# Borders between the stages of a hybrid decoder kernel: order of the last gate stores, early constants, weight loads inside the merge

## Chip, cores, metric

One core of a Trainium2 chip runs the whole program. The metric is the time of one execution in microseconds on the device; several timed runs are made of each kernel, and one further execution is profiled.

## What is computed

One layer of a decoder with three parallel branches, for a prompt of 2048 tokens and a sample group of 8 requests with 8 tokens each (2112 tokens in all, model width 1024, fp32). Cut to what matters here:

```python
h = rms_norm(x, p['norm_g'])
z = h @ p['w_in']                       # 1024 -> 7200 columns
a_x, a_g, b_s, b_g, c_q, c_kv, c_pe, c_g, gate_logits = split(z)
o_a = rg_lru(causal_conv(a_x)) * silu(a_g)        # branch a: RG-LRU, width 512
o_b = rwkv7_mix(b_s) * silu(b_g)                  # branch b: RWKV-7 recurrence, width 512
o_c = attend(q, ckv, c_pe) * silu(c_g)            # branch c: latent attention, width 512
g_a, g_b, g_c = split(sigmoid(gate_logits))       # three gates of 1024 columns
merged = g_a * (o_a @ w_oa) + g_b * (o_b @ w_ob) + g_c * (o_c @ w_oc)
y = x + merged @ w_out
```

The states of the branches (the last hidden state, convolution inputs, shifted columns, the recurrence's matrix states, the latents) are outputs too.

## The kernel before

Five engines run instruction streams of their own and meet through semaphores: PE (matmul), DVE and ACT (elementwise), POOL (elementwise and some transfers), SP (nearly all transfers). The program is a row of phases; each ends with a barrier over all engines (`Phase.__exit__`, L61), and SP reaches it only after the waits at the end of its own stream. Intermediate results go through DRAM between the phases: `zT` (branch inputs), `gT` (24 gate tiles of 128 columns), `oaT`, `obT`, `ocT` (branch outputs), `mT` (merged).

**Projection** (`trunk_phase`, L138). The tiles of 128 columns of z are worked on in pairs; each pair is computed by seven half-size products instead of eight (`ORDER`, L147), and DVE adds each product to the quarters of the two tiles that it belongs to (`adds`, L531; a quarter is one tile for one half of the tokens, 1056 of them). The last pairs are gate tiles: when both halves of a tile are summed, ACT makes tanh of the 2112 columns (`mix`, L387) and SP stores the tile (`store`, L248). After the loop over the pairs SP waits for DVE's copies of the branch states, issues 9 + 16 small stores of states (L270 to L280), stores the last two gate tiles (L281, L282), and waits until they have landed (L285).

**Prompt attention** (`prompt_attention_phase`, L1045) loads a pair of heads' keys into `kh` (two buffers, L1054) before PE's first score (L1180). **Sample attention** (`sample_attention_phase`, L1400) works through the eight requests; SP only loads a few new keys there (L1465 to L1470) and stores the result.

**Recurrence** (`rwkv_phase`, L1783). Twenty chunks (four per pair of heads, then the samples) go through a software pipeline, written out by hand per engine (`frame`). At its start SP issues 15 constants (L1891 to L1898; `lvl_f` are the level masks, cast by POOL at L1977, the others parameters and masks), then the three activations of chunk 0 (`load_inputs`, L1900), the low-rank input `wa` (1 MB for the prompt, L1951, and the sample columns, L1953), then both finished branches for the merge (`branches.load`, L2666, 4.2 MB each), then the activations of chunk 1. PE waits for all constants and for `prep` (L2044, L2045), that is for POOL's preparation, then multiplies `wa` (L2228). ACT waits for `prep` (L2327), squares the keys (L2335) and then takes PE's result (L2342, the log decay), on which everything else of the chunk hangs.

**Merge** (`merge_phase`, L2669). For each of 8 blocks of 128 columns, 15 units: three branches times five chunks of 424 tokens (the last 416). A unit is four matmuls into one of eight PSUM banks; DVE multiplies it by the gate (L2749) and adds it up (L2753). The weights of a block (three 256 KB matrices, one semaphore for all three, L2696) and its three gates (1056 KB each, L2700) have two buffers. POOL loads the recurrence's output, which the third branch needs (L2715).

**Output** (`out_phase`, L2756). Pairs of 128 tokens, seven products again; DVE makes sums of the token tiles (L2892) and, once, DVE and POOL make five sums of quarters of `w_out` (L2899, L2879). SP issues the first tokens (L2799), then the four quarters of `w_out` (1 MB each, L2811), then rows of x (L2806).

Of the kernel before, what the change touches and what calls it, by code (L numbers as in the profile page):

```python
# [12 lines left out]
P = 128  # L13
# [7 lines left out]
W = 512  # L21
# [116 lines left out]
def trunk_phase(nc, A, O, hT, ident, zT, gT, oaT, later, ahead):  # L138
# [15 lines left out]
    UPTO = {2: 2, 5: 4, 1: 6, 7: 7, 6: 8}  # L154
    with Phase(nc, "z") as p:
# [78 lines left out]
        with nc.Block() as block:  # L234
            @block.sync
            def _(sp):
# [24 lines left out]
                for q in range(NQ + 1):  # L261
                    if q:
# [18 lines left out]
                store(NQ, 0)  # L281
                store(NQ, 1)  # L282
                sp.wait_ge(xm_out, 16 * len(mixed))
                for u in range(4):
                    sp.wait_ge(st_out[u], 16 * max(stores[n] for q, r, n in ALL if buf(q, r) == u))  # L285
# [88 lines left out]
            def _(act):  # L374
# [85 lines left out]
                mix(NQ, 0)  # L460
                mix(NQ, 1)
# [583 lines left out]
def prompt_attention_phase(nc, A, O, ident, zT, qT, kT, v_d, ocT, outs, data):  # L1045
# [6 lines left out]
    with Phase(nc, "a") as p:  # L1052
        qb = p.sb("qb", [QK, 4, 2, P])
        kh = p.sb("kh", [QK, 2, 2, T])  # L1054
# [44 lines left out]
        with nc.Block() as block:  # L1099
            @block.sync  # L1100
            def _(sp):
                def heads(j):
                    for e in range(2):
                        sp.dma_start(kh[:, j % 2, e], kT[2 * j + e, :, 0:T]).then_inc(k_in[j % 2], 16)
# [64 lines left out]
            def _(pe):  # L1169
                def score(n, c):  # L1170
# [9 lines left out]
                    nc.tensor.matmul(S[x % 3][:, 0:cols], qb[:, m % 4, e], kh[:, j % 2, e, c * W:c * W + cols],  # L1180
# [219 lines left out]
def sample_attention_phase(nc, A, O, ident, ocT, data):  # L1400
# [4 lines left out]
    with Phase(nc, "s") as p:  # L1405
# [377 lines left out]
def rwkv_phase(nc, A, O, ident, zT, obT, oaT, ocT, branches):  # L1783
# [11 lines left out]
    with Phase(nc, "r") as p:  # L1795
        masks = p.sb("masks", [P, 4, C])
        lvl = p.sb("lvl", [P, LEVELS, 2, C], mybir.dt.uint8)
        bones = p.sb("bones", [P, P])
        cen = p.sb("cen", [P, P])
        bones2 = p.sb("bones2", [P, 2])  # L1800
        ident2 = p.sb("ident2", [P, C])
        scanm = p.sb("scanm", [P, W])
        prm = p.sb("prm", [P, 8, 4])
        tiny = p.sb("tiny", [P, 4])
        lora = p.sb("lora", [P, 4, P])
        wa = p.sb("wa", [P, T + W])
# [37 lines left out]
        c_in, prep, wa_in = p.sem("c_in"), p.sem("prep"), p.sem("wa_in")  # L1844
# [42 lines left out]
        with nc.Block() as block:  # L1887
            @block.sync
            def _(sp):
                cols = lambda a: a.rearrange("(q p) -> p q", p=P)  # L1890
                for dst, src in ((masks[:], A["rw_masks"]), (lvl_f, A["rw_levels"]), (bones[:], A["rw_bones"]),  # L1891
                                 (bones2[:], A["rw_bones2"]), (ident2[:], A["rw_ident2"]), (scanm[:], A["rw_scanm"]),
# [776 lines left out]
def merge_phase(nc, A, gT, obT, mT, branches):  # L2669

    with Phase(nc, "m") as p:
# [16 lines left out]
        with nc.Block() as block:  # L2688
            @block.sync
            def _(sp):  # L2690
                def loads(n):
# [5 lines left out]
                    if n >= 2:  # L2697
                        sp.wait_ge(took, NU * (n - 1))
# [312 lines left out]
```

## Time and profile before

| | |
|---|---|
| three timed runs | 4051.89, 4056.64, 4057.94 us; median 4056.64 |
| profiled execution | 4046.41 us |
| its span, first to last instruction | 4044.6 us |
| mean granted clock of PE | 0.967 of full |
| busy: PE, DVE, ACT, POOL | 92%, 51%, 33%, 11% of the span |
| moved by DMA | 293.48 MB |

A busy share is an average over all phases. The granted clock is the share of the full 2.4 GHz that the chip let PE have; 0.5 is its lower level. The start times below are microseconds from the first instruction.

### The profile page before, as it was taken

The numbers are of one execution on the slowest core, as the hardware profiler recorded it, in microseconds if no ns is written. First come the engines' busy times: TensorE is split into PE (matmuls) and PEld (weight loads), VectorE is DVE, ScalarE is ACT, GpSimd is POOL, SyncE is SP. The second block draws the span as 40 slices with busy tenths as digits, with TensorE's granted clock in tenths as the row PEclk, the third lists the DMA queues.
The fourth block names the chain that finished last, engine by engine and source line by source line (L and its number), as shares of the span: only waits on it lengthen the run. The fifth ranks groups of instructions, "written<-read, shape, count | busy, mean of one in ns | idle before, by whom it ended". The sixth has DMA issues, their size and how long they took to land. (4 is left out here: it accounts for less than half of the span.)

```text
span 4044.6 us, 72368 instructions
## 1 busy us (share of the span) xinstructions
PE 3723.9 (92%) x30307; PEld 2430.9 (60%) x30307; DVE 2076.8 (51%) x3717; ACT 1344.1 (33%) x2324; POOL 426.2 (11%) x580
## 2 busy tenths in 40 slices
PE   7879999999999999779999799977999998799899
PEld 4546666666666666456666555555777777455444
DVE  5863234444333333355666577764666664233353
ACT  4431012232233232244455455543555544000000
POOL 1000000000000000021111323302111121000000
PEclk9989999999999999899999899988999999899999
DMA  4422112222222222331211111003111111423342
GB/s 148 115 67 59 65 64 80 75 78 80 74 79 68 76 74 72 87 97 52 53 30 30 34 53 53 22 9 137 37 43 43 43 27 27 177 102 128 113 141 91
DMA packets 270300, 293.48 MB, mean 73 GB/s; under 512 B 81765, under 2 KB 229114, under 8 KB 255642
## 3 DMA queue, kind: packets, MB, share of 16 engines
q1 hardware_dynamic: 261066, 246.38, 19.6%
q0 software_dynamic: 8912, 42.48, 3.1%
q8 instruction: 242, 3.96, 0.4%
q14 instruction: 80, 0.66, 0.1%
HBM read 181.38 MB, written 107.42 MB: 71 GB/s over the span
## 5 line engine op out<-in xcount | busy, mean ns | idle before, releaser
L325 PE MATMUL z_acc<-z_hx,ahead_ws 128*128 128x352 f32 x1872 | 558.0, 459 | 0.0
L543 DVE TENSOR_TENSOR z_st<-z_st,z_acc 128x1056 f32<-128x1056 f32 x208 | 253.9, 1252 | 589.3 <-PE z_acc L325 589.3
L325 PEld LDWEIGHTS z_acc<-z_hx,ahead_ws 128*128 128x128 f32 x1872 | 355.7, 190 | 198.1
L325 PE MATMUL z_acc<-hT,ahead_ws 128*128 128x352 f32 x1248 | 376.9, 459 | 0.0
L325 PE MATMUL z_acc<-hT,ahead_wt 128*128 128x352 f32 x1248 | 373.4, 459 | 0.0
L1180 PE MATMUL a_S<-a_kh,a_qb 96*128 96x512 f32 (+3 forms) x640 | 289.5, 548 | 52.3 <-DMA a_kh<-kT 27.9
L325 PEld LDWEIGHTS z_acc<-hT,ahead_ws 128*128 128x128 f32 x1248 | 236.8, 190 | 135.5 <-issue 7.7
L325 PEld LDWEIGHTS z_acc<-hT,ahead_wt 128*128 128x128 f32 x1248 | 237.1, 190 | 132.1
L1528 PE MATMUL s_kn<-sd_wuk,s_ckT 128*128 128x512 f32 x528 | 287.9, 627 | 22.1 <-issue 17.0
L415 ACT ACTIVATE z_st<-z_acc 128x1056 f32<-128x1056 f32 x104 | 103.6, 1048 | 449.0 <-PE z_acc L325 449.0
L2729 PE MATMUL m_acc<-branches_o,m_wb 128*128 128x424 f32 (+1 forms) x640 | 230.1, 521 | 23.4 <-DMA m_wb<-in_w_ob 23.4
L2729 PEld LDWEIGHTS m_acc<-branches_o,m_wb 128*128 128x128 f32 x640 | 122.3, 191 | 129.7 <-issue 106.0
L1257 DVE CUSTOM_DVE_ANT_0 a_pr_l<-a_S,a_zm 128x512 f32<-128x512 f32 (+2 forms) x224 | 138.1, 629 | 117.6 <-PE a_S L1180 117.3
L1606 ACT ACTIVATE s_sq<-s_kn 128x512 f32<-128x512 f32 x264 | 155.9, 597 | 104.1 <-PE s_kn L1528 104.0
L1529 PEld LDWEIGHTS s_scp<-s_qabs,s_ckT 128*128 128x128 f32 x528 | 102.0, 193 | 129.8 <-issue 129.8
L1655 DVE TENSOR_REDUCE s_ssk<-s_sq 128x32 f32<-128x2048 f32 (+1 forms) x72 | 151.2, 2101 | 10.2 <-ACT s_sq L1606 9.8
L1180 PEld LDWEIGHTS a_S<-a_kh,a_qb 96*128 96x128 f32 x640 | 106.3, 202 | 79.2 <-issue 49.7
L1230 ACT ACTIVATE a_pr_l<-a_pr_l,a_nm 128x1024 f32<-128x1024 f32 (+7 forms) x128 | 122.5, 957 | 74.2 <-DVE a_nm L1264 58.7
L1189 PEld LDWEIGHTS a_tb<-ident,a_pr_l 128*128 128x128 f32 x800 | 98.2, 143 | 79.5 <-issue 58.9
L397 ACT ACTIVATE z_st<-z_st 128x2112 f32<-128x2112 f32 x24 | 47.1, 1964 | 271.4 <-DVE z_st L543 271.4
L1189 PE MATMUL a_tb<-ident,a_pr_l 128*128 128x128 f32 x800 | 117.8, 276 | 11.0 <-DVE a_pt_l L1220 9.9
L350 POOL DMA_DIRECT2D oaT<-z_tr x19 | 10.6, 558 | 1090.8 <-DVEq L598 1090.8
(411 smaller groups left out, 6389.4 us busy)
## 6 DMA issues: line engine op xcount, KB each, us to landing
ahead_wt<-in_w_in SPq DMA_DIRECT2D x52, 512.0 KB, 5.1
gT<-z_st SPq DMA_DIRECT2D x24, 1056.0 KB, 5.3
m_sg<-gT SPq DMA_DIRECT2D x24, 1056.0 KB, 9.2
zT<-z_xm SPq DMA_DIRECT2D x17, 1056.0 KB, 4.0
zT<-z_st SPq DMA_DIRECT2D x12, 1056.0 KB, 6.9
r_xs<-zT SPq DMA_DIRECT2D x48, 256.0 KB, 3.3
mT<-m_macc SPq DMA_DIRECT2D x8, 1056.0 KB, 5.4
p_xin<-in_x_prompt SPq DMA_DIRECT2D x16, 512.0 KB, 4.1
```

The costliest lines, as they stand in the source:

```text
L325: last = nc.tensor.matmul(acc[slot][:, i, 0:CH3], w[:, k], HB[m][:, k, i * CH3:(i + 1) * CH3], start=(k == 0), stop=(k == KH - 1))
L415: last = f(half(q, r, c), src, ACT.Copy)
L543: tt(y, y, src, ALU.add if sign > 0 else ALU.subtract).then_inc(took_v, 1)
L1180: nc.tensor.matmul(S[x % 3][:, 0:cols], qb[:, m % 4, e], kh[:, j % 2, e, c * W:c * W + cols], start=True, stop=True).then_inc(scored, 1)
L1189: last = nc.tensor.transpose(tb[x % 3][:, q], probs(n)[:, (4 * c + q) * P:(4 * c + q + 1) * P], ident[:])
L1230: nc.scalar.activation(probs(n)[:, k0:k1], probs(n)[:, k0:k1], ACT.Exp, bias=nm[:, n % 4:n % 4 + 1], accum_out=ls[:, n // 2 % 2, n % 2, c ...
L1257: nc.vector.tensor_tensor_reduce(out=probs(n)[:, c * W:c * W + cols], in0=S[x % 3][:, 0:cols], in1=mask, scale=1.0, scalar=NEG, op0=ALU.ad ...
L1528: nc.tensor.matmul(kn[page % 3][:], ckT[:, r, q], wuk[:], start=True, stop=True).then_inc(kn_done, 1)
L1529: nc.tensor.matmul(scp[r][:, q], ckT[:, r, q], qabs[:, b:b + 1].rearrange("p a n -> p (a n)"), start=(q == 0), stop=False, skip_group_chec ...
L1606: nc.scalar.activation(sq[:, r, q], kn[page % 3][:], ACT.Square).then_inc(squared, 1)
L1655: nc.vector.tensor_reduce(own, sq[:, r, 0:k].rearrange("p a (h d) -> p a h d", h=H), AX.X, ALU.add).then_inc(summed, 1)
L2729: last = nc.tensor.matmul(acc[x % 8][:, 0:tn], wb[:, n % 2, k, q], o[k][:, q, t0:t0 + tn], start=(q == 0), stop=(q == 3))
```

## The change

Four edits at the borders of the phases:

1. The last pair's tanh and stores are made by quarters (tile, half of the tokens), each as soon as its last add is done; the small stores of states come after them. Before the barrier SP waits for the quarters.
2. A buffer of 16 KB per partition, `early.pool`, lives from prompt attention to the end. First it holds one of the two key buffers; at the start of the sample phase, 14 of the 15 constants of the recurrence and the prompt's part of `wa` are loaded into it. The level masks stay in the recurrence, behind the activations of chunk 0. PE's wait for POOL's preparation moves to its first statistics product.
3. In the merge each weight matrix has a semaphore of its own; gates go through a ring of four slots, each loaded when the gate four places before it is used up; one of the two sums lies in `early.pool`.
4. The four quarters of `w_out` are loaded into a buffer of their own (`last.wo`) during the merge, after the store of its fourth block; the output's token sums lie where the branches were.

```diff
+    QUARTERS = ((1, 0), (0, 1), (0, 0), (1, 1))
+    LAST_ADD = {(1, 0): 1, (0, 1): 3, (0, 0): 7, (1, 1): 8}
...
+                for x, (r, c) in enumerate(QUARTERS):
+                    sp.wait_ge(gate_r, len(gates) - 2 + x + 1)
+                    u, t0 = buf(NQ, r), 1 + c * HALF
+                    sp.dma_start(gT[tiles(NQ)[r] - 29, :, c * HALF:(c + 1) * HALF], st[:, u, t0:t0 + HALF]).then_inc(st_out[u], 16)
                 sp.wait_ge(sh_cp, 1)
...
-                store(NQ, 0)
-                store(NQ, 1)
...
-                mix(NQ, 0)
-                mix(NQ, 1)
+                for r, c in QUARTERS:
+                    act.wait_ge(took_v, 8 * (NQ - 1) + LAST_ADD[r, c])
+                    t0 = 1 + c * HALF
+                    part = st[:, buf(NQ, r), t0:t0 + HALF]
+                    f(part, part, ACT.Tanh, scale=0.5).then_inc(gate_r, 1)
...
-        kh = p.sb("kh", [QK, 2, 2, T])
+        kh = [early.keys(), p.sb("kh", [QK, 2, T])]
...
                 sp.wait_ge(const_set, 2)
+                early.load(sp, A, zT)
...
+class Early:
...
+        self.pool = ctx.enter_context(nc.sbuf_tensor("early_pool", [P, 2 * T], F32))
...
+    def load(self, sp, A, zT):
...
+        for dst, src in ((self.masks, A["rw_masks"]), (self.bones, A["rw_bones"]),
...
+            sp.dma_start(dst, src, allow_slow_non_contiguous=True).then_inc(self.c_in, 16)
+        sp.dma_start(self.wa[:, 0:T], zT[20, :, 1:T + 1]).then_inc(self.wa_in, 16)
...
-                for dst, src in ((masks[:], A["rw_masks"]), (lvl_f, A["rw_levels"]), (bones[:], A["rw_bones"]),
...
-                    sp.dma_start(dst, src, allow_slow_non_contiguous=True).then_inc(c_in, 16)
...
                 load_inputs(0)
-                sp.dma_start(wa[:, 0:T], zT[20, :, 1:T + 1]).then_inc(wa_in, 16)
+                sp.dma_start(lvl_f, A["rw_levels"]).then_inc(lvl_in, 16)
                 sp.wait_ge(prep, 1)
...
-                g.wait_ge(c_in, 15 * 16)
+                g.wait_ge(c_in, 14 * 16)
+                g.wait_ge(lvl_in, 16)
...
-                pe.wait_ge(c_in, 15 * 16)
-                pe.wait_ge(prep, 5)
+                pe.wait_ge(c_in, 14 * 16)
...
                 def input_stats(n):
+                    if n == 0:
+                        pe.wait_ge(prep, 5)
...
-        sg = p.sb("sg", [P, 2, 3, TT])
+        sg = p.sb("sg", [P, 4, TT])
-        macc = p.sb("macc", [P, 2, TT])
+        macc = [early.pool[:, 0:TT], p.sb("macc", [P, TT])[:]]
...
+                def weights(n):
+                    if n >= KD:
+                        return
                     u = n % 2
                     if n >= 2:
                         sp.wait_ge(prod, NU * (n - 1))
                     for k, w in enumerate((A["w_oa"], A["w_oc"], A["w_ob"])):
-                        sp.dma_start(wb[:, u, k], w[0].rearrange("(k p) n -> p k n", p=P)[:, :, n * P:n * P + P]).then_inc(w_in[u], 16)
...
+                        sp.dma_start(wb[:, u, k], w[0].rearrange("(k p) n -> p k n", p=P)[:, :, n * P:n * P + P]).then_inc(w_in[u][k], 16)
+
+                def gate(x):
+                    if x >= 3 * KD:
+                        return
+                    if x >= 4:
+                        sp.wait_ge(took, 5 * (x - 3))
+                    sp.dma_start(sg[:, x % 4], gT[ORDER[x % 3] * KD + x // 3]).then_inc(g_in[x % 4], 16)
+
+                weights(0)
+                for x in range(3):
+                    gate(x)
+                sp.wait_ge(prod, 5)
+                weights(1)
+                gate(3)
+                for n in range(KD):
                     for k in range(3):
...
+                        gate(3 * n + k + 4)
+                    weights(n + 2)
                     sp.wait_ge(m_r, 10 * (n + 1))
...
+                    sp.dma_start(mT[n], macc[n % 2]).then_inc(stored[n % 2], 16)
+                    if n == 3:
+                        last.load(sp, A)
...
-                    pe.wait_ge(w_in[n % 2], 48 * (n // 2 + 1))
...
+                        if c == 0:
+                            pe.wait_ge(w_in[n % 2][k], 16 * (n // 2 + 1))
...
-        wo = p.sb("wo", [P, KD, D])
+        wo, wo_in = last.wo, last.wo_in
-        ms = p.sb("ms", [P, 2, 5, KH, P])
+        ms = branches.o[:, 0].rearrange("p k t -> p (k t)")[:, 0:10 * KH * P].rearrange("p (u a k n) -> p u a k n", u=2, a=5, k=KH)
...
                 load_m(0)
-                for q in (0, 3, 1, 2):
-                    r, c = q // 2, q % 2
-                    sp.dma_start(B(r, c), A["w_out"][0, r * W:(r + 1) * W, c * W:(c + 1) * W].rearrange("(k p) n -> p k n", p=P)).then_inc(wo_in[q], 16)
                 load_x(0)
```

## Rows read from the trace of the kernel before

**Rows 1.** The page, part 1: PE's busy time, share of the span, instructions.

```profile
PE 3723.9 (92%) x30307; PEld 2430.9 (60%) x30307; DVE 2076.8 (51%) x3717; ACT 1344.1 (33%) x2324; POOL 426.2 (11%) x580
```

**Rows 2.** Windows view: stretch, length, busy (records) by engine, granted clock, DMA.

```profile
3473.00:3480.00 7.00, 6.30 (x13) 3.30 (x14) 0.60 (x1) 0.00 (x0) 0.00 (x0) 0.69 0.81 338
3480.00:3600.00 120.00, 120.00 (x340) 64.29 (x339) 41.71 (x70) 0.00 (x0) 0.00 (x0) 1.00 0.34 120
```

**Rows 3.** Timeline, projection to prompt attention: start, us, engine, line [idle before <-releaser].

```profile
1650.40 1.25 DVE L543 TENSOR_TENSOR z_st<-z_st,z_acc 128x1056 f32<-128x1056 f32 x1 [5.85 <-PE z_acc L325]
...
1651.69 1.96 ACT L397 ACTIVATE z_st<-z_st 128x2112 f32<-128x2112 f32 x1 [5.13 <-DVE z_st L543]
...
1652.08 0.40 SPq L273 DMA_DIRECT2D out_p_shift<-later_shT  x1
...
1660.86 0.83 SPq L256 DMA_DIRECT2D gT<-z_st  x2
...
1678.73 10.89 PE L1180 MATMUL a_S<-a_kh,a_qb 96*128 96x512 f32 x20 [27.92 <-DMA a_kh<-kT]
```

**Rows 4.** SP's waits, 1640 to 1690: us in total, times, longest.

```profile
SPq L285 <- DMA gT<-z_st: 5.7, 2, 3.1
```

**Rows 5.** Timeline, sample attention to recurrence.

```profile
2725.85 0.35 SPq L1898 DMA_DIRECT2D r_masks<-in_rw_masks  x1
...
2733.59 1.52 SPq L1910 DMA_DIRECT2D r_xs<-zT  x3
...
2735.88 0.82 POOL L1977 CAST r_lvl<-r_GM 128x768 uint8<-128x768 f32 x1 [7.66 <-DMA r_lora<-in_rw_a]
...
2739.91 0.72 ACT L2335 ACTIVATE r_sq<-r_xs,r_prm 128x512 f32<-128x512 f32 x1 [27.71 <-DMA r_xs<-zT]
...
2743.38 2.04 PE L2228 MATMUL r_r<-r_wa,r_lora 64*128 64x512 f32 x2 [22.01 <-DMA r_wa<-zT]
2745.46 0.69 ACT L2342 ACTIVATE r_lw<-r_r,r_prm 128x512 f32<-128x512 f32 x1 [4.82 <-PE r_r L2228]
```

**Rows 6.** Timeline, recurrence to merge.

```profile
3455.61 0.37 SPq L2696 DMA_DIRECT2D m_wb<-in_w_oa  x1
...
3457.12 2.31 SPq L2700 DMA_DIRECT2D m_sg<-gT  x3
...
3473.70 30.43 PE L2729 MATMUL m_acc<-branches_o,m_wb 128*128 128x424 f32 x80 [23.37 <-DMA m_wb<-in_w_ob]
...
3478.74 0.60 DVE L2749 SCALAR_TENSOR_TENSOR m_macc<-m_sg,m_acc 128x424 f32<-128x424 f32 x1 [26.58 <-PE m_acc L2729]
```

**Rows 7.** DMA view, 3452 to 3476: issues, KB each, median us from issue to landing.

```profile
m_ob<-obT POOLq DMA_DIRECT2D x1, 4224.0 KB, 17.4
m_sg<-gT SPq DMA_DIRECT2D x3, 1056.0 KB, 20.9
m_wb<-in_w_oa SPq DMA_DIRECT2D x1, 256.0 KB, 3.2
m_wb<-in_w_oc SPq DMA_DIRECT2D x1, 256.0 KB, 5.1
m_wb<-in_w_ob SPq DMA_DIRECT2D x1, 256.0 KB, 17.1
```

**Rows 8.** Timeline, merge to output.

```profile
3828.35 3.10 DVE L2892 TENSOR_TENSOR y_ms<-y_mb 128x512 f32<-128x512 f32 x5 [11.01 <-DMA y_mb<-mT]
...
3831.38 9.28 PE L2863 MATMUL y_acc<-y_wo,y_ms 128*128 128x512 f32 x16 [15.28 <-DMA y_wo<-in_w_out]
```

**Rows 9.** DMA view, 2722 to 2745.

```profile
r_GM<-in_rw_levels SPq DMA_DIRECT2D x1, 384.0 KB, 3.0
...
r_wa<-zT SPq DMA_DIRECT2D x1, 32.0 KB, 7.3
```

**Rows 10.** DMA view of the whole program: medians from issue to landing.

```profile
m_sg<-gT SPq DMA_DIRECT2D x24, 1056.0 KB, 9.2
...
y_wo<-in_w_out SPq DMA_DIRECT2D x4, 1024.0 KB, 10.2
```

More of the change, by code:

```diff
@@ L2666, in load, with __init__, merge_phase @@
             eng.dma_start(self.o[:, k], src.rearrange("n p t -> p n t")).then_inc(self.o_in[k], 16)
-def merge_phase(nc, A, gT, obT, mT, branches):
+class Last:
+    def __init__(self, nc, ctx):
+        self.wo = ctx.enter_context(nc.sbuf_tensor("last_wo", [P, KD, D], F32))
+        self.wo_in = [ctx.enter_context(nc.semaphore(f"last_wo_in{k}")) for k in range(4)]
+    def load(self, eng, A):
+        KH = KD // 2
+        for q in (0, 3, 1, 2):
+            r, c = q // 2, q % 2
+            eng.dma_start(self.wo[:, KH * r:KH * r + KH, W * c:W * c + W],
+                          A["w_out"][0, r * W:(r + 1) * W, c * W:(c + 1) * W].rearrange("(k p) n -> p k n", p=P)).then_inc(self.wo_in[q], 16)
+def merge_phase(nc, A, gT, obT, mT, branches, early, last):
     with Phase(nc, "m") as p:
@@ L2681, in merge_phase @@
         ORDER = (0, 2, 1)
-        g_in = [p.sems(f"g{u}_in", 3) for u in range(2)]
-        w_in, stored = p.sems("w_in"), p.sems("st")
+        g_in = p.sems("g_in", 4)
+        w_in, stored = [p.sems(f"w{u}_in", 3) for u in range(2)], p.sems("st")
         prod, took, m_r = p.sem("prod"), p.sem("took"), p.sem("mr")
@@ L2753, in _, with out_phase @@
                             nc.vector.tensor_tensor(m, m, out, ALU.add).then_inc(m_r, 1)
-def out_phase(nc, A, O, mT, outs):
+def out_phase(nc, A, O, mT, outs, branches, last):
     KH = KD // 2
@@ L2954, in build @@
             trunk_phase(nc, A, O, hT, ident, zT, gT, oaT, later, ahead)
-        with ExitStack() as middle:
-            data = SampleData(nc, middle)
-            prompt_attention_phase(nc, A, O, ident, zT, qT, kT, v_d, ocT, later.outs, data)
-            sample_attention_phase(nc, A, O, ident, ocT, data)
-        with ExitStack() as back:
-            branches = Branches(nc, back)
-            rwkv_phase(nc, A, O, ident, zT, obT, oaT, ocT, branches)
-            merge_phase(nc, A, gT, obT, mT, branches)
-        out_phase(nc, A, O, mT, later.outs)
+        with ExitStack() as around:
+            early = Early(nc, around)
+            with ExitStack() as middle:
+                data = SampleData(nc, middle)
+                prompt_attention_phase(nc, A, O, ident, zT, qT, kT, v_d, ocT, later.outs, data, early)
+                sample_attention_phase(nc, A, O, ident, zT, ocT, data, early)
+            with ExitStack() as back:
+                branches = Branches(nc, back)
+                rwkv_phase(nc, A, O, ident, zT, obT, oaT, ocT, branches, early)
+                last = Last(nc, back)
+                merge_phase(nc, A, gT, obT, mT, branches, early, last)
+                out_phase(nc, A, O, mT, later.outs, branches, last)
 OUT = {"y_p": (1, T, D), "y_s": (DB, TS, D), "p_lru_h": (1, 1, 512), "p_lru_conv": (1, 1, 3, 512),
```

74 lines of the change are left out of this document (36 added, 38 removed).

## The prediction

> **What bounds the kernel now.** I read the page first: TensorE (PE) is busy for 92% of the span [rows 1], so time can only be won where PE stands idle or where a phase is one chain of small steps. The windows view says that the merge is full once it runs: 120 us busy of 120, at the full granted clock, 340 matmul records; eight of them make one unit (one branch, 424 tokens), so a unit takes 120 / 340 x 8 = 2.82 us [rows 2]. Inside the phases the change has nothing to win; I therefore read the timeline at the borders, and beside it the DMA view and SP's waits. Four borders can be seen to stand still.
>
> At the first (projection to prompt attention) SP issues 25 small stores and only then the last two gate tiles, and must see those landed before the barrier: small stores from 1652.08, gates at 1660.86, PE again at 1678.73 [rows 3]; SP's waits put 5.7 us to the gates' landing [rows 4]. At the third (sample to recurrence) SP issues 15 constants before the first activations: POOL casts the masks when the last constant is there, ACT starts on the activations 4.03 us later, PE starts when the low-rank input is in, and the chain's first elementwise result is ACT's at 2745.46 [rows 5]. At the fourth (recurrence to merge) PE starts at 3473.70, on the last of three weight matrices [rows 6]; the first had taken 3.2 us and the third 17.1 [rows 7]. At the fifth (merge to output) PE waits for output weights until 3831.38, though the tokens were there at 3828.35 [rows 8].
>
> **The change, part by part.** The sum is made against the profiled execution: span 4044.6 us, 4046.41 us in all. That is 10.2 us under the median of the timed runs, 4056.64; I carry the difference in microseconds over to the median.
>
> *First border.* Before, SP is free when the gates have landed: 1660.86 + 0.83 + 5.7 = 1667.4 [rows 3, 4]. After, three quarters are stored while PE still works. The last needs the last add (ends 1651.65) and a tanh over half the elements: half of 1.96, so 1651.69 + 0.98 = 1652.67 [rows 3]. Its issue takes half of 0.83, 0.4 us, and then come the small stores, 1660.86 - 1652.08 = 8.8 us: SP ends at 1661.9, and the quarter lands behind that work (5.7 us for four times the bytes bounds it). Nobody waits for the small stores before the end of prompt attention. Gain 1667.4 - 1661.9 = 5.5 us; between 4.0, if issuing beside a store is slower, and 6.5. The next loads then run as they do now. The additional ACT instructions lie under the adds.
>
> *Second border.* 14 constants and the 1 MB low-rank input are issued by SP when the sample phase has set its own constants: about 7.7 us of issue, as now from 2725.85 to 2733.59 [rows 5]. Queued behind them on SP are the new keys of the third request, which wait for the first request's sums anyway. Cost nothing; without that cover, 7.7 us. The two halves of the prompt's keys only change address: nothing.
>
> *Third border.* SP begins with the three activation loads (1.52 us of issue), then the level masks at about 2727.4, the sample columns at about 2727.9, then both branches. POOL, whose queue holds the cast and what follows, now waits for the level masks. The trace has no such transfer behind three 256 KB loads. The bounds are 3.0 us (the same masks, nearly alone) and 7.3 us (the sample columns behind 1.8 MB) [rows 9]; I take 4.8, nearer the lower end, since 768 KB lie in front. So masks at 2732.2. Cast to ACT's first square is 4.03 us and from there to the log decay 0.72 and a gap of 0.02 [rows 5], hence 2732.2 + 4.8 = 2737.0 in place of 2745.46: gain 8.5 us, between 6.0 and 10.3. PE's first product may be as late as 2727.9 + 7.3 + 2.1 = 2737.3 without undoing this. The wait for the other POOL work, moved to PE's statistics, comes later than ACT's own wait for the same and costs nothing.
>
> *Fourth border.* PE now waits for one matrix at a time. The first lands at 3455.61 + 3.2 = 3458.8 [rows 6, 7]: gain 3473.70 - 3458.8 = 14.9 us. Does it last? The first unit takes 3478.74 - 3473.70 = 5.0 us on the slow start (granted clock 0.69 of full in these 7 us, a mixture of 1.2 and 2.4 GHz) [rows 2, 6]. PE can fill eight banks before DVE must free one: until 3458.8 + 5.0 + 7 x 2.82 = 3483.5. DVE needs the gates: the median one lands 20.9 us after an issue near 3457.6, so 3478.5 [rows 6, 7]. The second matrix had taken 5.1 us and is needed after five units, at 3475; the third matrix and the recurrence's output (17.1 and 17.4 us) are there by 3473.7, when PE starts now, and needed after ten units, at 3489. No stall: 14.9 us. Lower bound, if the first matrix lands like the second: 13.
>
> A rule speaks against this step. The Trainium skill (DMA: Bandwidth & Descriptors, section Queues, rings and completion order) says that each DMA engine takes turns between the queues that have work, a packet at a time, and that completion does not follow the order of issue. By that rule the first matrix could be caught by POOL's 4.2 MB as the third was; the sum would be 16.4 us instead of 31.3. The trace agrees for the third matrix and not for the first.
>
> In the merge, gates go through four slots instead of six. A gate is issued when the one four before it is used up, three gates or 15 x 2.82 = 42 us ahead of need, and takes 9.2 us [rows 10]: nothing. The 4 MB of output weights go out after the fourth block's store, ahead of later gates on SP: 4 us of issue, and even four median landings in a row, 41 us [rows 10], end, with the gate behind them, within the 56 us that the next gate has (20 units): nothing. The separate weight waits on PE are satisfied by then: nothing.
>
> *Fifth border.* The weights are there, so PE starts on the first token sum: 3828.35 plus a fifth of 3.10, 3829.0 [rows 8]; gain 2.4 us, between 1.5 and 3.5 (the tokens now have other loads behind them). What would be late next are the three weight sums on DVE and two on POOL; they move earlier by more than PE does.
>
> Sum: 5.5 + 8.5 + 14.9 + 2.4 = 31.3 us. Span 4013.3, from the median 4025.3.
>
> **The rivals.** *First matrix late.* If the engines spread POOL's transfer over it, PE starts at 3473.5 as before, and 14.9 us are lost: 4056.64 - 16.4 = 4040.2. Against it stands the row of 3.2 us, with the same issues in the same order; for it the row of 17.1 [rows 7].
>
> *Next inputs late.* The second chunk's activations stand on SP behind 8.4 MB of branches, and ACT's chain may wait for these instead of the masks, so that the 8.5 us are given back at the second chunk: 4033.8. Against it: the branches are issued about 8 us earlier as well, and so are these.
>
> *Both.* Only the first and fifth borders remain, 7.9 us: 4048.7, which the measurement cannot tell from no change (0.2%, 8.1 us).
>
> *Slower: four slots.* If gates should land so late that DVE and then PE wait at each of the 20 gates that recycle a slot, the merge loses. It starts to lose beyond 42 us from issue to landing, and loses more than everything won from 42 + 31.3 / 20 = 43.6 us; at 44.1 us it is 20 x 2.1 = 42 us lost, 10.7 us slower: 4067.3. Against it: 9.2 us [rows 10]; even beside the 4.2 MB transfer the median was 20.9 [rows 7].
>
> **How the numbers follow.** Forecast 0.72; first matrix late 0.12; next inputs late 0.06; both 0.06; four slots 0.04. Faster by over 0.2%: 0.72 + 0.12 + 0.06 = 0.90; same 0.06; slower 0.04. The likeliest case gives 4025.3; with its terms at their best ends (6.5 + 10.3 + 14.9 + 3.5 = 35.2) 4021.4, and with the timed runs' downward spread of 4.75 us and some 2.5 us for a PE that starts at full clock after a shorter gap, 4014. The upper end takes in the late first matrix, 4040.2, and the runs' upward spread of 1.3: 4042.
>
> **What would show it.** In the new timeline: SP's first load of prompt attention about 5.5 us closer to the last add; the cast on POOL about 6.4 us after SP's first issue of the recurrence, not 10.0; the merge's first matmul about 3.3 us after SP's first weight issue, not 18.1, and no idle PE until the ninth unit; the output's first matmul 0.7 us after the first token sum begins, and a DMA share above the old one in the sample's first slices only. Wrong would be: a merge that starts with the third matrix, PE gaps at the ninth unit, a second chunk that begins no earlier, or a slower merge between its borders.

## The result, and the profile after

| | before | after |
|---|---|---|
| median of the timed runs | 4054.26 us (4 runs, 4049.48 to 4057.94) | 4019.45 us (4 runs, 4015.89 to 4025.47) |
| ratio | | 0.9916, 95% interval 0.9899 to 0.9934 |
| profiled execution, and its span | 4046.41, 4044.6 us | 4021.59, 4019.8 us |
| a later comparison of the same two (9 and 5 runs) | 4047.93 us | 4024.44 us, ratio 0.9946 (0.9932 to 0.9960) |

The change makes the kernel faster: 34.8 us by the medians of the first comparison, 24.8 by the two profiled spans, 23.5 in the later comparison. The forecast was 31.3. Why three measurements of one change differ by 11 us turned out to be the larger question; the kernel before alone gives medians of 4047.93 and 4054.26 here, and the changed one 4019.45 and 4024.44. First the borders.

**First border.** Timeline of the changed kernel, as in [rows 3] (start, us, engine, line, what, idle before).

```profile
1649.05 1.25 DVE L551 TENSOR_TENSOR z_st<-z_st,z_acc 128x1056 f32<-128x1056 f32 x1 [5.85 <-PE z_acc L330]
...
1651.44 0.32 SPq L275 DMA_DIRECT2D gT<-z_st  x1
1651.81 0.46 SPq L279 DMA_DIRECT2D out_p_shift<-later_shT  x1
...
1660.64 0.30 SPq L286 DMA_DIRECT2D out_s_lru_conv<-later_lruT  x1
1662.18 0.33 SPq L1119 DMA_DIRECT2D a_qb<-qT  x1
...
1673.31 11.09 PE L1188 MATMUL a_S<-early_pool,a_qb 96*128 96x512 f32 x20 [23.86 <-DMA early_pool<-kT]
```

The last quarter goes out before the small stores, and SP reaches its first load 13.13 us after the start of the last add instead of 18.15. PE's first score comes 24.26 us after it, 4.07 earlier than before (28.33). What fills the border now is SP's issue of small stores, 1651.81 to 1660.94.

**Third border.** Timeline, as in [rows 5].

```profile
2717.35 0.42 DVE L1742 SCALAR_TENSOR_TENSOR s_oS<-s_oS,sd_cg 128x256 f32<-128x256 f32 x1
...
2720.86 1.30 SPq L1937 DMA_DIRECT2D r_xs<-zT  x3
...
2726.91 0.82 POOL L2005 CAST r_lvl<-r_GM 128x768 uint8<-128x768 f32 x1 [3.70 <-DMA r_GM<-in_rw_levels]
...
2730.33 0.72 ACT L2364 ACTIVATE r_sq<-r_xs,early_pool 128x512 f32<-128x512 f32 x1 [23.16 <-POOL early_pool L2012]
2730.96 0.67 ACT L2371 ACTIVATE r_lw<-r_r,early_pool 128x512 f32<-128x512 f32 x1
```

The cast starts 6.05 us after SP's first issue instead of 10.03, and the first log decay 13.61 us after the last elementwise instruction of the sample phase (2717.35) instead of 23.10.

**Fourth and fifth border.** First the timeline at the merge's start, as in [rows 6]; then the DMA view of 3446 to 3460, as in [rows 7]; then the timeline at the output's start, as in [rows 8].

```profile
3447.24 0.38 SPq L2742 DMA_DIRECT2D m_wb<-in_w_oa  x1
...
3452.21 18.09 PE L2785 MATMUL m_acc<-branches_o,m_wb 128*128 128x424 f32 x46 [10.24 <-DMA m_wb<-in_w_oa]
3467.37 2.61 DVE L2805 SCALAR_TENSOR_TENSOR early_pool<-m_sg,m_acc 128x424 f32<-128x424 f32 x5 [23.57 <-DMA m_sg<-gT]
```

```profile
m_wb<-in_w_oa SPq DMA_DIRECT2D x1, 256.0 KB, 4.9
m_wb<-in_w_oc SPq DMA_DIRECT2D x1, 256.0 KB, 5.2
m_wb<-in_w_ob SPq DMA_DIRECT2D x1, 256.0 KB, 16.7
```

```profile
3806.50 3.10 DVE L2944 TENSOR_TENSOR branches_o<-y_mb 128x512 f32<-128x512 f32 x5 [10.94 <-DMA y_mb<-mT]
3807.25 5.18 PE L2915 MATMUL y_acc<-last_wo,branches_o 128*128 128x512 f32 x8 [12.94 <-DVE branches_o L2944]
```

PE now starts on the first matrix, 4.97 us after SP's first weight issue instead of 18.09. DVE waits for the gates until 3467.37, and PE fills its banks meanwhile and does not stop. The output starts 0.75 us into the first token sums; before, it waited 3.03 us for weights.

The ledger is read from the same instruction in both profiles (after minus before, us):

| instruction | shift | what the stretch gave |
|---|---|---|
| projection's last add | -1.35 | nothing changed so far: two executions |
| first score | -5.42 | -4.07, first border |
| last elementwise instruction of the sample phase | -5.01 | +0.41 |
| first log decay (chunk 1) | -14.50 | -9.49, third border |
| log decay of chunk 3 | -6.35 | **+8.15** |
| last store of the recurrence | -8.37 | -2.02 |
| merge's first product | -21.49 | -13.12, fourth border |
| merge's last add | -21.78 | -0.29 |
| output's first product | -24.13 | -2.35, fifth border |
| end of the span | -24.8 | -0.67 |

The row in bold is not in the forecast: two chunks after the third border, 8.15 of the 9.49 us are gone. The reason shows when the granted clock is read there. Below is ACT's timeline in the kernel before, chunks 2 and 3, and then the windows view (stretch, length, busy and records of PE, weight loads, DVE, ACT, POOL, then the granted clock).

```profile
2769.76 0.69 ACT L2342 ACTIVATE r_lw<-r_r,r_prm 128x512 f32<-128x512 f32 x1 [3.31 <-PE r_r L2228]
...
2801.17 0.69 ACT L2342 ACTIVATE r_lw<-r_r,r_prm 128x512 f32<-128x512 f32 x1 [5.54 <-PE r_r L2228]
```

```profile
2755.00:2766.00 11.00, 5.43 (x66) 3.75 (x68) 4.02 (x6) 0.37 (x2) 2.62 (x2) 0.50 0.86 350
2768.00:2773.00 5.00, 4.95 (x132) 3.16 (x132) 2.96 (x5) 2.36 (x4) 0.75 (x1) 1.00 0.00 0
```

The same two views of the changed kernel:

```profile
2756.64 0.69 ACT L2371 ACTIVATE r_lw<-r_r,early_pool 128x512 f32<-128x512 f32 x1 [5.28 <-PE r_r L2255]
...
2794.82 0.69 ACT L2371 ACTIVATE r_lw<-r_r,early_pool 128x512 f32<-128x512 f32 x1 [5.55 <-PE r_r L2255]
```

```profile
2755.00:2766.00 11.00, 10.18 (x136) 6.75 (x136) 4.63 (x8) 5.03 (x8) 2.15 (x2) 0.50 0.01 1
2766.00:2772.00 6.00, 6.00 (x100) 5.53 (x100) 1.96 (x3) 1.51 (x3) 0.38 (x1) 0.50 0.01 3
2774.00:2790.00 16.00, 14.23 (x414) 12.20 (x414) 9.45 (x15) 8.02 (x12) 3.31 (x3) 1.00 0.16 52
```

Behind chunk 2's log decay stand level products (those of chunk 1, as the pipeline is written). Before, PE reached them at 2769.66, just after the full clock (2.4 GHz) had come at 2767.4. After, it reaches them at 2756.53, 13 us sooner by the trace's time and 8 us sooner counted from the end of the sample phase, and does them at 0.50, the lower level, until 2772.6: 38.18 us from chunk 2 to chunk 3 instead of 31.41. That is 6.78 of the 8.15 us; the other 1.37 go in chunk 1, which is at half clock in both kernels. The head start is spent at half speed, and the full clock even comes later than before: 55.3 us after the sample phase's last elementwise instruction instead of 45.0.

### The profile page after: what moved, and what is told of

It reads as the page before. It is cut to its first block and busy times, and to the rows that moved or that the text cites. A ratio compares the mean times of both kernels' runs of the same rounds, so it can differ in the third digit from the quotient of the medians.

```text
span 4019.8 us, 72387 instructions
## 1 busy us (share of the span) xinstructions
PE 3727.5 (93%) x30307; PEld 2434.0 (61%) x30307; DVE 2075.6 (52%) x3717; ACT 1344.9 (33%) x2326; POOL 426.3 (11%) x580
## 5 line engine op out<-in xcount | busy, mean ns | idle before, releaser
L1188 PE MATMUL a_S<-early_pool,a_qb 96*128 96x512 f32 (+3 forms) x320 | 147.9, 560 | 45.3 <-DMA early_pool<-kT 23.9
L1188 PE MATMUL a_S<-a_kh,a_qb 96*128 96x512 f32 (+3 forms) x320 | 141.5, 535 | 3.9 <-DMA a_qb<-qT 3.9
```

The source lines that it names most:

```text
L1188: nc.tensor.matmul(S[x % 3][:, 0:cols], qb[:, m % 4, e], kh[j % 2][:, e, c * W:c * W + cols], start=True, stop=True).then_inc(scored, 1)
```

## The experiments

All are edits of the changed kernel, except where it is said. The table holds what each profile shows: PE's first score after the start of the projection's last add; the log decays of chunks 1 and 3 after the sample phase's last elementwise instruction; the time from the third to the twentieth log decay; the merge's first product after SP's first weight issue; and the timed runs (ratio to the kernel before on the same chip). The kernel called late here is the one with late constants.

| kernel | score | chunk 1 | chunk 3 | 3rd to 20th | merge | median us | ratio (95%) |
|---|---|---|---|---|---|---|---|
| before | 28.33 | 23.10 | 78.81 | 572.69 | 18.09 | | 1 |
| after | 24.26 | 13.61 | 77.47 | 568.90 | 4.97 | 4019.45 | 0.9916 (0.9899 to 0.9934) |
| after, again | 23.42 | 13.72 | 77.49 | 568.75 | 4.26 | 4024.44 | 0.9946 (0.9932 to 0.9960) |
| all weights | 23.21 | 13.65 | 77.50 | 570.48 | 18.27 | 4037.91 | 0.9965 (0.9951 to 0.9979) |
| late | 23.68 | 23.20 | 78.92 | 577.69 | 2.92 | 4028.47 | 0.9944 (0.9928 to 0.9961) |
| busy PE | 23.47 | 13.61 | 67.47 | 570.64 | 2.74 | 4012.18 | 0.9908 (0.9892 to 0.9925) |
| late and busy PE | 23.60 | 25.61 | 81.08 | 570.51 | 2.95 | 4025.39 | 0.9942 (0.9927 to 0.9958) |
| states early | 16.29 | 14.46 | 77.98 | 581.34 | 4.57 | 4020.22 | 0.9921 (0.9905 to 0.9938) |
| statistics apart | 23.26 | 13.65 | 74.65 | 556.11 | 2.80 | 4000.79 | 0.9886 (0.9871 to 0.9901) |
| statistics apart, again | 23.47 | 13.85 | 77.53 | 556.23 | 2.75 | 3999.73 | 0.9874 (0.9857 to 0.9891) |
| late, statistics apart | 23.50 | 22.62 | 78.34 | 556.23 | 4.42 | 4004.15 | 0.9890 (0.9875 to 0.9905) |
| before, statistics apart | 28.76 | 22.37 | 78.14 | 557.76 | 17.29 | 4024.89 | 0.9941 (0.9927 to 0.9954) |
| three edits together | 16.00 | 13.96 | 67.76 | 555.13 | 2.95 | 3983.17 | 0.9839 (0.9825 to 0.9852) |

**All weights: is it the third matrix that held PE?**

```diff
-                        if c == 0:
-                            pe.wait_ge(w_in[n % 2][k], 16 * (n // 2 + 1))
+                        if c == 0 and k == 0:
+                            for j in range(3):
+                                pe.wait_ge(w_in[n % 2][j], 16 * (n // 2 + 1))
```

> The changed kernel, but PE waits for all three weight matrices of a block before the block's first product, as before the change. Theory (the third matrix was what held PE at the fourth border): the merge's first product comes about 17 to 18 us after SP's first weight issue instead of 4.97, and the time rises by 12 to 13 us, to about 4032. Rival (the first gates, which land 20 us after that issue, set the merge's pace, so that an early PE only fills its banks): the first product is as late, but the merge ends at most 3 us later, about 4020 to 4022.

Timeline and DMA view of this kernel at the merge's start:

```profile
3449.76 0.38 SPq L2742 DMA_DIRECT2D m_wb<-in_w_oa  x1
...
3468.03 4.22 PE L2786 MATMUL m_acc<-branches_o,m_wb 128*128 128x424 f32 x6 [23.54 <-DMA m_wb<-in_w_ob]
```

```profile
m_wb<-in_w_oa SPq DMA_DIRECT2D x1, 256.0 KB, 2.7
m_wb<-in_w_oc SPq DMA_DIRECT2D x1, 256.0 KB, 12.3
m_wb<-in_w_ob SPq DMA_DIRECT2D x1, 256.0 KB, 17.1
```

It was: PE starts at 18.27, when the third matrix is there, although the first had taken 2.7 us. From SP's first weight issue to the merge's last add it takes 361.33 us, against 347.73 with separate waits and 361.14 before. So 13.4 to 13.6 us arrive at the merge's end, and the rival, by which the gates set the pace, falls. The median stands 18.5 and 13.5 us above the two of the changed kernel, which were not run beside it; the theory had 12 to 13, and its 4032 was 6 us too low.

**Late: what are the early constants worth?** The call moves out of the sample phase, back to the head of the recurrence.

```diff
-                early.load(sp, A, zT)
...
+                sp.dma_start(lvl_f, A["rw_levels"]).then_inc(lvl_in, 16)
+                early.load(sp, A, zT)
                 load_inputs(0)
-                sp.dma_start(lvl_f, A["rw_levels"]).then_inc(lvl_in, 16)
+                sp.dma_start(wa[:, 0:T], zT[20, :, 1:T + 1]).then_inc(wa_in, 16)
```

> The changed kernel, but the 14 constants and the 1 MB of low-rank input are issued in the recurrence again, in the old order (constants and level masks, activations, low-rank input). Theory (the second chunk runs at half the clock until a moment that the earlier start does not move, so most of the third border's gain is given back there): the first log decay is 9 us later after the last elementwise instruction of the sample phase (23 instead of 13.6), but the third chunk's log decay only 1 to 2 us later (about 79 instead of 77.5), and the time 4020 to 4022. Rival (the 9.5 us of the border are kept and what was lost in the recurrence is chance): the third chunk's log decay at 86 to 87, the time about 4029.

The profile says what the theory said: chunk 1 is 9.6 us later, chunk 3 only 1.45. The time says 4028.5, the rival's number; but its ratio, 0.9944, is that of the unaltered changed kernel in the later comparison, 0.9946. By time alone this run decides nothing. In its profile another 8.8 us are lost between the third and the twentieth log decay, where the edit does nothing. One part of the theory does not hold: the moment of the full clock moves with the edit. It comes 45.0 us after the sample phase's last elementwise instruction here, as before the change, and 55.3 with early constants.

**Busy PE: is it the clock?** Throwaway products fill PE's gaps in chunk 1.

```diff
+                def warm(*cols):
+                    for n in cols:
+                        mm(go[:, 0:n], ident[:], scanm[:, 0:n], start=True, stop=True)
...
                 def lora_w(n):
                     if n == 0:
+                        warm(W, W, W, W)
```

There are five more such calls, ahead of the second low-rank product (640 columns), the input's statistics (256), the bonus (1024), the scales (256) and the two halves of the gram products (1024 and 256).

> The changed kernel, with throwaway products on PE in the gaps of the recurrence's first chunk (the identity times the scan mask, into a bank that nobody has read yet): about 8 us of them before the first low-rank product and 0.5 to 4 us in each later gap. Theory (PE's half clock holds the second chunk): PE is granted the full clock within some 7 us of the phase's start, as after the first border, and the third chunk's log decay comes 66 to 71 us after the last elementwise instruction of the sample phase instead of 77.5; the time falls by 7 to 11 us, to 4008 to 4013. Rival one (the second chunk waits for its activations, which stand behind both branches): 77 and no change, 4019. Rival two (the clock does not answer, and the added products delay the chain by the part that does not fit the gaps): 79 to 82, 4021 to 4024.

Windows view of this kernel from the end of the sample phase, and ACT's log decays of chunks 2 and 3:

```profile
2721.00:2726.00 5.00, 4.19 (x6) 1.87 (x7) 0.00 (x0) 0.00 (x0) 2.37 (x5) 0.53 0.61 193
2726.00:2733.00 7.00, 4.22 (x11) 1.72 (x10) 0.31 (x1) 1.30 (x2) 3.15 (x10) 0.97 1.05 372
2733.00:2743.00 10.00, 10.00 (x20) 4.78 (x19) 4.93 (x8) 6.71 (x10) 3.15 (x3) 0.51 1.01 427
2743.00:2790.00 47.00, 40.03 (x1078) 31.41 (x1076) 28.04 (x46) 19.29 (x30) 9.76 (x8) 1.00 0.21 80
```

```profile
2754.34 0.69 ACT L2385 ACTIVATE r_lw<-r_r,early_pool 128x512 f32<-128x512 f32 x1 [2.06 <-PE r_r L2262]
...
2785.75 0.69 ACT L2385 ACTIVATE r_lw<-r_r,early_pool 128x512 f32<-128x512 f32 x1 [5.54 <-PE r_r L2262]
```

The full clock comes with the throwaway products (1.00 from 2743 on, against 2772), and with it chunk 3 comes 10.0 us sooner. The time, 4012.18, lies in the theory's 4008 to 4013. The next activations still stand behind both branches here, so "next inputs late" is out as the cause, and the products added delay nothing that can be seen.

**Late and busy PE: the border's worth with the clock out of the way.** The two edits together, the throwaway products now identity times identity and three times as many at the start.

```diff
-                        mm(go[:, 0:n], ident[:], scanm[:, 0:n], start=True, stop=True)
+                        for _ in range(n // P):
+                            mm(go[:, 0:P], ident[:], ident[:], start=True, stop=True)
...
-                        warm(W, W, W, W)
+                        warm(*[W] * 12)
+                        pe.wait_ge(c_in, 14 * 16)
```

> The changed kernel with the constants and the low-rank input loaded in the recurrence again, as in the kernel with late constants, and throwaway products on PE from the phase's start, here identity times identity, as long as the constants take, and in the gaps of the first chunk. Theory (the early constants are worth 9.5 us, and PE's half clock in the second chunk hid most of it): with the clock up in both, the third chunk's log decay comes about 9.5 us later than in the kernel with busy PE (77 against 67.5 us after the last elementwise instruction of the sample phase), and the time is about 9 us above that kernel's 4012, 4021. Rival (early constants are worth 1.4 us whatever the clock): 69, and 4013 to 4014.

PE's timeline at the first low-rank product, and the windows view of the two stretches behind it:

```profile
2743.29 2.04 PE L2263 MATMUL r_r<-early_pool 64*128 64x512 f32 x2 [6.90 <-DMA early_pool<-zT]
```

```profile
2742.00:2758.00 16.00, 14.71 (x46) 10.47 (x47) 5.15 (x8) 7.40 (x11) 3.14 (x3) 0.50 1.01 423
2759.00:2801.00 42.00, 35.97 (x983) 29.90 (x982) 24.66 (x39) 16.31 (x26) 8.48 (x7) 1.00 0.14 46
```

Chunk 3 comes at 81.08, 13.6 us after the kernel with early constants and busy PE. That is more than the 9.5 expected, for two reasons. Chunk 1 itself is 12.0 us later: its low-rank input landed 2.4 us later than in the late kernel (the sample columns took 9.9 us from issue to landing, 7.5 there), and PE stood idle for it for 6.90 us, behind the throwaway products. And after this gap chunk 1 runs at half clock again, 24.06 us to chunk 2's log decay instead of 22.46. From chunk 2 to chunk 3, at the full clock in both, each takes 31.41 us. So the 12.0 us of chunk 1 are all still there at chunk 3 where PE is fast in chunk 2, and only 1.45 of 9.6 where it is not. The rival's 69 us is out. The time, 4025.39, is 13.2 us above busy PE's (on another chip; the ratios differ by 0.0034, 13.8 us); the theory had 9.

**States early: what is left of the first border?** The 25 small stores, and the transposes and copies that they need, move ahead of the last quarters.

```diff
+                        if m == 2 and q == NQ:
+                            pe.wait_ge(r_a, 2 * len(LRU_STEPS))
+                            pe.wait_ge(mix_r, len(mixed))
+                            nc.tensor.transpose(gate[0][0:80, 0:P], sh[:, 0:5].rearrange("p i n -> p (i n)"), ident[:])
...
                 sp.wait_ge(sh_cp, 1)
                 for i in range(DB + 1):
...
+                for x, (r, c) in enumerate(QUARTERS):
```

> The changed kernel, with the transposes and copies of the branch states made during the last pair of tiles and the 25 small stores issued before the last quarters, where SP waits anyway. Theory (after the change the first border lasts as long as SP's 9 us of small stores): SP's first load of prompt attention about 7 us after the start of the projection's last add instead of 13.1, PE's first score about 18 instead of 24.3, the time lower by 5.5 to 6, 4013 to 4014. Rival (the landing of the last quarter, 2.7 us beside the small stores, is no better than the whole tile's 5.7, or the next keys land later): SP's first load at 10, the time lower by 0 to 3 us.

```profile
1649.21 1.25 DVE L552 TENSOR_TENSOR z_st<-z_st,z_acc 128x1056 f32<-128x1056 f32 x1 [5.85 <-PE z_acc L330]
1655.38 0.33 SPq L1121 DMA_DIRECT2D a_qb<-qT  x1
...
1665.50 2.04 PE L1190 MATMUL a_S<-early_pool,a_qb 96*128 96x512 f32 x2 [16.33 <-DMA early_pool<-kT]
```

The border did what the theory said: SP at 6.17 us, PE at 16.29, another 7 to 8 us. The median did not follow; the ratio, 0.9921, lies between the two of the changed kernel. At the end of the sample phase this profile is 7.7 us ahead of the changed kernel's; from the third to the twentieth log decay it loses 12.4. Its windows view shows five stretches like these in the sixteen prompt chunks:

```profile
2830.20:2833.20 3.00, 3.00 (x46) 2.67 (x44) 0.92 (x2) 0.60 (x1) 0.00 (x0) 0.50 0.03 5
2932.60:2935.60 3.00, 3.00 (x49) 2.67 (x46) 0.94 (x2) 0.60 (x1) 0.00 (x0) 0.50 0.00 0
...
3239.80:3242.80 3.00, 3.00 (x48) 2.62 (x44) 0.94 (x2) 0.60 (x1) 0.00 (x0) 0.50 0.00 0
```

PE counts as busy throughout and is at half clock. A chunk takes 33.50 us from log decay to log decay, and 35.0 to 35.2 with such a stretch in it. Each begins some 9 to 10 us after a log decay, behind the same products. So do all such stretches in the prompt chunks of the eight profiles with this order of products: 18 of them, none to five in a profile, each 9.2 to 9.7 us after a log decay and at most 0.5 us behind the last of these products. The kernel with busy PE is the one without any. PE's timeline ahead of the second of them:

```profile
2928.68 0.95 PE L2269 MATMUL r_r<-early_pool,r_sq 128*128 128x2 f32 x8
...
2931.11 1.02 PE L2294 MATMUL r_go<-early_pool,r_gsq 128*128 128x2 f32 x8 [0.29 <-ACT r_oT L2419]
```

These are the statistics of the input and of the output, products with two columns each.

**After, again; statistics apart; three edits together.** The first is the changed kernel unaltered, as a reference. The second moves the output's statistics behind the next level product:

```diff
                     x(2)
-                    on(o, output_stats)
                     if a is not None:
                         tokens(a, AR[:, a % 2, 0], AT)
                     on(c, link, 4)
                     y(3)
+                    on(o, output_stats)
```

> The changed kernel once more, unaltered, on the chip of the runs beside it. In the traces so far the time from the third to the twentieth log decay of the recurrence was 568.9 to 581.3 us and went with the number of stretches of some 3.4 us at half the granted clock in it (one to five, each costing the chunk about 1.5 us). Theory (this is what makes runs of one kernel differ): 568 to 575 us here, the time 4014 to 4024. Rival (the changed kernel is always at the low end and the variants lose by their own edits): 569 within 1 us.

> The changed kernel, with the statistics products of the output (two columns each) two steps later in PE's order, so that they do not follow closely behind the statistics products of the input. In the traces each half-clock stretch in the body of the recurrence begins 9.1 to 9.5 us after a log decay, behind these two groups. Theory (the pair of groups is what lets the clock fall): at most one such stretch in the first sixteen chunks, third to twentieth log decay 566 to 570 us, the time lower by 0 to 6 us, near 4015. Rival (the stretches have another cause): one to five of them at the same place, 569 to 581 us, and no change, 4019.

> The changed kernel with the three edits together: busy PE in the first chunk, states stored early, output statistics two steps later. Theory (each takes away what bounds its stretch, and nothing else is late): PE's first score 16 to 17 us after the start of the projection's last add, the third chunk's log decay 67 to 68 us after the sample phase, third to twentieth log decay at most 571 us; the time 7 + 7 + 0 to 4 us lower, 4002 to 4006. Rival (what is won early is given back in half-clock stretches of the recurrence): the first two as said, but 575 us or more for the third, and 4009 to 4013.

The reference took 568.75 us from the third to the twentieth log decay, which both theories allow: it decides nothing between them, and its timed runs (median 4024.44) lie at the upper end of the first comparison's and above. The other two do decide. With the statistics apart no stretch at half clock is left in the chunks (windows view):

```profile
2770.00:3000.00 230.00, 218.86 (x6259) 182.43 (x6258) 154.80 (x275) 117.57 (x191) 42.86 (x40) 1.00 0.13 40
3000.00:3200.00 200.00, 191.88 (x5447) 159.87 (x5449) 138.09 (x248) 104.15 (x172) 38.50 (x36) 1.00 0.14 43
3200.00:3400.00 200.00, 184.92 (x4972) 154.41 (x4971) 122.98 (x213) 100.78 (x170) 40.93 (x39) 1.00 0.14 30
```

It was worth far more than the theory gave it: 556.11 us, not 566 to 570, and 4000.8 us. Three things came together. A chunk without any stretch fell from 33.50 to 33.04 us, of which 0.35 are waits that PE no longer has, 0.29 of them for the output's squares; over sixteen chunks 0.46 us make 7.4. The stretches are gone. And the tail from the twentieth log decay to the recurrence's last store takes 71.74 us instead of 80.11; its first 59.9 us are at the full clock, where the changed kernel has two stretches at half clock. How much of the last is clock and how much order was not separated. Nor was what ended the stretches: the edit sets the two groups of products apart and also takes away 0.35 us of idle PE in each chunk.

The three edits together reach 3983.17 us, under the forecast of 4002 to 4006 by about what the statistics brought beyond theirs, and 64.8 us under the kernel before on that chip. The border, the first chunks and the body show the numbers that each edit had alone. It is the best kernel of this study.

**The change itself, in a quiet recurrence.** With the statistics apart, the kernels before and after, and the changed one with late constants, were run beside each other.

> The kernel before, with only the output's statistics products two steps later in PE's order. Theory (the body of the recurrence is quiet with this edit, so that the whole change can be weighed without the half-clock stretches): third to twentieth log decay 555 to 557 us instead of 572.7, and the time lies above the same edit in the changed kernel by the borders as the traces showed them: 4.1 to 5.1 for the first, 1.3 to 4 for the third as the third chunk sees it, 13.1 to 15.3 for the fourth, 2.4 for the fifth, 21 to 27 us in all, 4022 to 4028. Rival (the third border's 9.5 us are kept once the body is quiet): 30 to 33 us, 4031 to 4034.

> The changed kernel with the output's statistics two steps later and with the constants loaded in the recurrence again. Theory (the early constants start the first chunk 9.5 us sooner, and PE's half clock gives most of it back by the third): the third chunk's log decay 77 to 79 us after the last elementwise instruction of the sample phase, against 74.65 with early constants, and the time 2 to 4 us above that kernel's. Rival (the 9.5 us are kept): 84, and 9 to 10 us above.

> The changed kernel with the output's statistics two steps later, unaltered from its first run, as the reference of the two kernels beside it on this chip. Expected by the theory that its recurrence is quiet: again 556 us within 1 from the third to the twentieth log decay, and timed runs of 3999 to 4006. By the rival (its first run was a lucky one): 565 us or more and 4010 or more.

The whole change is worth 4024.89 - 3999.73 = 25.2 us, 24.5 by the profiled spans (4022.5 and 3998.0): inside the theory's 21 to 27, and not the rival's 30 to 33. Late constants cost 4.4 us, a little over the theory's 2 to 4 and half of the rival's 9 to 10. Of this, chunk 3 shows 0.8 against the kernel beside it; the rest lies in the tail (2.7) and at the merge's start (4.42 against 2.75), where no step of the edit is. Against the first run of the same kernel chunk 3 shows 3.7: there the full clock came 48.9 us after the sample phase's last elementwise instruction and here 55.1, so that one kernel's chunk 3 differs by 2.9 us from profile to profile. All three bodies took 556 to 558 us; the kernel before, with 557.76, is a little over the theory's 555 to 557.

By the two profiles, the 24.5 us lie at the borders like this: first 5.3, second -1.5, third 0.6 at chunk 3 (8.5 at chunk 1), fourth 14.5, fifth 1.9. Another 3.4 us come between chunk 3 and the merge, where the change does nothing.

## Why the prediction was right, and where it was not

**First border**, 5.5 forecast: 4.07 at PE in the pair of profiles, 4.1 to 5.1 over the profiles with the change; 5.0 at SP. The mechanism is as told. Issuing beside a store was slower (eight small stores 3.55 us, 3.20 before), the lower bound that I had named, and PE's key loads landed 1 us later (8.4 us, 7.4 before). Quarters and order were not tried apart.

**Second border**, nothing forecast: from the first score to the end of the sample phase it takes 0.41 us more in the pair of profiles. Over eight profiles with the early loads that stretch took 1044.0 to 1048.2 us, over five without them 1043.1 to 1047.5: no cost that can be told from the scatter.

**Third border**, 8.5 forecast: 9.49 at the first log decay. The level masks landed in 4.3 us, not 4.8, and cast to squares took 3.42 instead of 4.03. But the step "hence 2732.2 + 4.8 = 2737.0 in place of 2745.46: gain 8.5 us" failed as a price for the whole program: it ended the count at chunk 1. What bounds chunk 2 is PE, and PE stayed at half clock while the work came 13 us sooner, so 1.3 us are left at chunk 3 in the profiled pair and 0.6 in the quiet one; by time the early constants are worth 4.4 there. The 13 us are by the trace's time; 5 of them were won before the recurrence. One rival, at 0.06, gave the 8.5 us back at the second chunk, and that is where they went; but its cause, the activations behind the branches, is not the one: ACT had its squares done (2750.64, 0.72 us) before PE took up the low-rank product at 2754.53. The view that would have warned of it stood in the trace of before: granted clock 0.50 up to 2766, and chunk 2 begun only as it rose. That the full clock would come 10 us later with an earlier start could not be read there, and its reason stays open.

**Fourth border**, 14.9 forecast: 13.12 in the pair. The first matrix landed in 4.9 us there, and in 2.7 in others; PE started 2.74 to 4.97 us after the issue over ten profiles, around the 3.3 of the forecast, so the gain is 13.1 to 15.4 us, against the 13 to 14.9 of the prediction. What decides the landing was not found: in a quick one (2.75) and in the slowest, POOL's transfer was issued 0.46 us behind SP's. By the rule of the Trainium skill (DMA: Bandwidth & Descriptors, section Queues, rings and completion order), engines take turns between queues and completion does not follow the order of issue; over the thirteen profiles the traces agree for the third matrix (15.6 to 17.1 us), for the second in some (3.2 to 12.9), and the first, at 2.7 to 4.9, was never caught. No stall followed, and four slots lost nothing: from its first product to its last add the merge took 342.76 us, 343.05 before; its gates landed in 5.2 us by the median.

**Fifth border**, 2.4 forecast, 2.35 in the pair of profiles; it was not undone by itself.

So the sum of 31.3 should have been about 25, as the quiet pair shows, and the third border's term is what was too large: without it the other three make 22.8. The forecast of 4025.3 lies close to the measured 4019.45 because the comparison then made came out 10 us better than the change is worth. That closeness is luck: it covers a sum that was some 6 us too large.

What the 10 us are can be seen in part. The record has the mean granted clock of most timed runs, and the time goes with it: in 26 runs of the kernel before, those at 0.968 took 4042.5 and 4043.3 us, those at 0.964 4054.6 and 4057.3; in nine of the changed kernel, 4015.89 at 0.971, 4024.4 and 4028.4 at 0.967. Over all 26 it is some 3 us for each 0.001 (correlation -0.89); 0.001 of the mean is 8 us of the span at half clock, and that much lost work, at full clock, is 4 us: the size fits. So the spread of one kernel's runs goes with the time that PE spends at half clock; a correlation does not show that it is the cause of all of it. Where in the program these times lie, only the one profiled execution of each kernel tells: the chunks from the third to the twentieth log decay took 568.75 to 581.34 us in the eight profiles of kernels without the edit to the statistics. They are not all of it: the changed kernel with the edit, whose chunks have no such stretch in two profiles, still took 3992.66 to 4005.62 us in eight runs, at 0.974 to 0.970.

## What to carry to other kernels

A gain at the start of a pipeline is worth what is left of it where the engine that bounds the steady state takes over: follow it two or three steps on, and read the granted clock there. Where a kernel gives different gains from one comparison to the next, compare the same inner stretch over all profiles before explaining the difference by the edit. At a border, ask which issues nobody waits for, and put them where their queue idles anyway.

## What the runs showed of the hardware

PE can count as busy without a break in the profile and stay at the lower clock: 10.18 of 11 us and 6.00 of 6, at 0.50 throughout, in the changed kernel's chunk 2. The Trainium skill (TensorE: Matmul & The Clock Gate, Part 1) has it that the slow clock is the default and that sustained activity releases it; busy PE agrees (first throwaway product at 2721.81, full clock from 2725.7, then 0.51 again from 2733 to 2743), this stretch of the changed kernel only late, at 2772.6.

An earlier start of the same work moved the full clock later: 45.0 us after the sample phase's last elementwise instruction in the four profiles with the constants in the recurrence and no throwaway products, 55.1 to 55.4 us in five of the six with early constants, 48.9 in the sixth. Why was not found.

In the prompt chunks the clock also falls in the middle of a chain that is busy for 31.97 us of 33.50 (the changed kernel, 2894.3 to 2927.8), there always behind the two groups of two-column products, and a change in the order of one group ended it in all five profiles that had the edit. Each fall cost a chunk about 1.5 us. Behind the prompt chunks the clock falls in other places too.
